# Moving adaLN's steps, the gate matmuls and the ScalarE and VectorE work of an RG-LRU behind other columns

## The chip, the cores and the metric

One Trainium2 chip, one core. The time is the device time of one execution in microseconds; lower is better. The whole network (two blocks, 256 positions) is one program, and all five engine programs run side by side, held together by semaphores alone.

## The reference

Two layers of a first block, then one layer of a second. What the change touches is the mixer of the first block's second layer (RG-LRU) and one matrix product of the second block that is computed far ahead, piece by piece (adaLN's `mod`):

```python
def rglru_mixer(h, w_in, conv_w, conv_b, w_a, b_a, w_x, b_x, lam, w_out):   # 10 blocks of 128 channels
    gate, xr = jnp.split(h @ w_in, 2, axis=-1)
    xr = causal_dwconv(xr, conv_w, conv_b)                # 4 taps
    r = sigmoid(blockwise(xr, w_a) + b_a)
    i = sigmoid(blockwise(xr, w_x) + b_x)
    log_a = -RG_C * r * softplus(-lam)
    a = exp(log_a)
    b = sqrt(-expm1(2.0 * log_a)) * (i * xr)
    hs = scan(a, b)                                       # h_t = a_t h_(t-1) + b_t
    return (gelu(gate) * hs) @ w_out
...
mod = c_act @ ada_w[l] + ada_b[l]                         # 1024 x 6144, of one row
```

## The kernel before

**Data.** Channels lie on the 128 partitions and the 256 positions along a row. Every weight matrix is read once from HBM in tiles of 128 x 1024 fp32 (512 KB): a "column" is 128 output channels by all 1024 inputs. A product in nearly full fp32 is made of three fast ones: each tile is split into a high part (`whi`, a ScalarE copy) and a low part (`wlo`, a VectorE subtraction), the input likewise (`hh`, `hl`), and TensorE adds hh·whi + hl·whi + hh·wlo, so a column is 24 matmuls of 128x128 by 128x256 into one PSUM bank. `project(w, [a, b])` makes two columns together: at each input tile k three matmuls of column a, then three of column b, so it needs both weights from its start.

**Order.** `weight_order` (line 113) lists all tiles as TensorE wants them, and SyncE starts their DMAs in that order into a ring of nine slots (`NR`); a DMA waits until TensorE is done with the tile nine places ahead. The high parts lie in seven buffers (`NS`). ScalarE and VectorE make the parts in the order of the list when their programs come to `feed(c)`: ScalarE up to place c+6 of the list, VectorE up to c+5 (`AHEAD` is 5, line 177; the loops stand at lines 1041 and 1565). What stands in an engine's program between two feeds runs before the later one. At the end of a residual both engines feed from the first weight of the next layer.

**adaLN.** Its matrix is 48 tiles in the same list, two for each of 24 steps. They aren't split: `mod_step` runs four narrow fp32 matmuls on each pair straight from the ring and adds into one PSUM bank that is held through a row of eight steps; at the eighth ScalarE copies the row to `mrow`. `mod_turn` is TensorE's four transposes of that copy into another bank, which VectorE adds to `mod`. The second row begins and ends in the RG-LRU: `ADA_RG` says behind which columns its eight steps come, and now the turn is asked for at each gate column and happens behind the first one after the eighth step.

**The RG-LRU.** Columns 10 to 19 of `rg_w_in` are the recurrent branch, 0 to 9 the gate. TensorE starts 10, 11, 12 on the unscaled input (`early`) while the norm's statistics are made. VectorE then makes the scaled input (`h_tiles`), lifts the three early columns and runs their taps (three each), and comes to the first `feed` of the layer only behind them. For each recurrent column m: ScalarE's `last_tap`, VectorE's `taps`; `ri(m)` is TensorE's two fp32 block matmuls and ScalarE's two sigmoids, and the table `RI` says behind which column it comes (places 0 to 9 are columns 10 to 19, places 10 to 19 the gates 0 to 9). GpSimd multiplies i by xr. ScalarE's `decays` are a tanh and two exps for each m, VectorE's `sizes` follow, ScalarE's `roots` (a square root for two m), VectorE's `scan`, ScalarE's `gelus` of the gate, VectorE's `times_gate`, ScalarE's `high_of_y`, VectorE's `low_of_y`. Each is put behind a gate column by a small table in the loops below, and the rest into the loop over the ten k of `rg_w_out`. That product runs k outermost over all eight outputs, so it takes all eight PSUM banks before its first matmul, the one of adaLN's row among them.

**Banks.** TensorE's `take` goes round the eight banks, leaves out the held one and waits until the last reader of the bank it comes to has given it back: for a recurrent column that is VectorE's last tap.

Sums go through a few helpers, so the profile has one line for each engine and operation: L470 TensorE, L1037 ScalarE, L1552 and L1558 VectorE, L1942 the scan, L573 the turn.

Of the kernel before, what the change touches and what calls it, by code (L numbers as in the profile page):

```python
# [79 lines left out]


ADA_IN = ((), (2, 5, 8, 11, 14, 17, 19, 21))
ADA_RG = ((5, 7, 9), (1, 3, 5, 7, 8))
YW = ((0, 2), (2, 2), (4, 2), (6, 4))


# [9 lines left out]

RI = ((), (), (), (), (), (), (0, 1), (2, 3), (4, 5), (6,), (7,), (8,), (9,)) + ((),) * 7

# [118 lines left out]
def build(nc, d, out):  # L221
    with ExitStack() as ctx:
# [241 lines left out]
        def tensor_program(e):  # L464
# [83 lines left out]
            def mod_step():  # L548
                n = ada["n"]
                ada["n"] += 1  # L550
                r, k = n // 8, n % 8
                if k == 0:
                    take(("ada", r))
                p = ps[where["ada", r]]
                for z in range(2):
                    c = number["ada_w", n, z]
                    landed[c % NR].wait_ge(e, c)
                    ada_dve.wait_ge(e, "sc32")
                    for y in range(2):
                        g = 2 * z + y  # L560
                        t = mm(p[32 * g:32 * g + 32, :], sc32[:, k, :], ring[c % NR][:, 4 * y:4 * y + 4, :], k == 0, k == 7)
                    t.then_inc(*through.up(c))
                if k == 7:
                    give(("ada", r), ada_act, r)
                    ada["late"] = r
# [118 lines left out]
            def conv_ffn(l):  # L684
                w = f"ffn_w_in{l}"
                n = 2 * l + 1
                early(n)
                for i, at in enumerate(EARLY[n]):
                    give(at, ff_dve, (l, "lift", i))
                project(w, [23, 2], n)  # L690
                give((w, 23), ff_dve, (l, "g", 1))
                give((w, 2), ff_dve, (l, "u", 2))
                for m in range(2, 22):
                    if m > 2:
                        project(w, [m], n)
                        give((w, m), ff_dve, (l, "u", m))
                    project(w, [m + 22], n)
                    give((w, m + 22), ff_dve, (l, "g", m))
                    if m in ADA_IN[l]:
                        mod_step()  # L700

                def also(m):
                    mod_turn()

                residual(2 * l + 2, f"ffn_w_out{l}", 22, pair(hidh[l], hidl[l]), lambda k: ff_dve.wait_ge(e, (l, "lo", k)), also)

            def rglru():
                def ri(m):
                    p, p2 = take(("r", m)), take(("i", m))
                    wab_in.wait_ge(e, "all")  # L710
                    rg_dve.wait_ge(e, ("x", m))
                    mm(p[:, 0:T], wab[:, m, :], xr[:, m, :]).then_inc(*rg_pe.up(("r", m)))
                    mm(p2[:, 0:T], wab[:, 10 + m, :], xr[:, m, :]).then_inc(*rg_pe.up(("i", m)))
                    give(("r", m), rg_act, ("r", m))
                    give(("i", m), rg_act, ("i", m))

                early(2)
                for m in range(3):
                    give(("rg_w_in", m + 10), rg_dve, ("lift", m))
                for m in range(3, 10):  # L720
                    if m == 3:
                        project("rg_w_in", [13, 14], 2)
                    elif m > 4:
                        project("rg_w_in", [m + 10], 2)
                    give(("rg_w_in", m + 10), rg_dve, ("x", m))
                    for i in RI[m]:
                        ri(i)
                    if m in ADA_RG[0]:
                        mod_step()
                for m in range(10):  # L730
                    project("rg_w_in", [m], 2)
                    give(("rg_w_in", m), rg_act, ("gate", m))
                    mod_turn()
                    if m in ADA_RG[1]:
                        mod_step()
                    for i in RI[m + 10]:
                        ri(i)
                outs = [take(("rg_w_out", m)) for m in range(8)]
                at = [(k, m) for k in range(8) for m in range(8)] + [(k, m) for m in range(8) for k in (8, 9)]
                for k, m in at:  # L740
                    c = number["rg_w_out", 0, k]
                    j = turn[c] % NS
                    low.wait_ge(e, c)
                    rg_dve.wait_ge(e, ("yl", k))
                    o, a, z = outs[m][:, 0:T], whi[j][:, m, :], wlo[c % NR][:, m, :]
                    mm(o, a, yh[:, k, :], k == 0, False)
                    mm(o, a, yl[:, k, :], False, False)
                    t = mm(o, z, yh[:, k, :], False, k == 9)
                    if k == 9:
                        t.then_inc(*rg_pe.up(("out", m)))  # L750
                        give(("rg_w_out", m), resid, (3, m))
                    elif m == 7:
                        t.then_inc(*through.up(c))
# [278 lines left out]
        def scalar_program(e):  # L1032
# [241 lines left out]
            def rglru():  # L1274
# [42 lines left out]
                def high_of_y(m):  # L1317
                    rg_dve.wait_ge(e, ("y", m))
                    act(yh[:, m, :], gate[:, m, :], ACT.Copy).then_inc(*rg_act.up(("yh", m)))
# [8 lines left out]
                for m in range(10):  # L1328
                    feed(tail("rg_w_in", m))
                    act(gate[:, m, :], out_of("rg_w_in", m), ACT.Copy).then_inc(*rg_act.up(("gate", m)))  # L1330
                    if m in ADA_RG[1]:
                        mod_step()
                    for i in RI[m + 10]:
                        ri(i)
                    decays({2: (0, 1, 2, 3), 3: (4, 5, 6), 4: (7, 8, 9)}.get(m, ()))
                    roots({5: (0, 2), 6: (4, 6), 7: (8,)}.get(m, ()))
                    gelus({7: (0, 1), 8: (2, 3, 4), 9: (5, 6, 7, 8, 9)}.get(m, ()))
                    if m > 7:
                        high_of_y(m - 8)
                for k in range(10):  # L1340
                    if k < 8:
                        high_of_y(k + 2)
                    if k == 9:
                        for m in range(8):
                            resid.wait_ge(e, (3, m))
                            gather(3, m)
                            high_of_h(3, m)
                    feed(number["rg_w_out", 0, k])
# [198 lines left out]
        def vector_program(e):  # L1547
# [322 lines left out]
            def conv_ffn(l):  # L1870
# [24 lines left out]
                for m in range(22):  # L1895
                    if m > 1:
                        feed(tail(w, m))
                    taps(zu_, "u", m, out_of(w, m) if m > 1 else zl[l][:, 2 * m, :], m)
                    if m:
                        feed(tail(w, m + 22))  # L1900
                    taps(zg_, "g", m + 22, out_of(w, m + 22) if m else zl[l][:, 1, :], m)
                    behind(m)
                    if m in ADA_IN[l]:
                        mod_step()
                behind(22)
                behind(23)

# [12 lines left out]
            def rglru():  # L1920
# [41 lines left out]
                        mod_step()  # L1962
                for m in range(10):
                    feed(tail("rg_w_in", m))
                    mod_turn()
                    if m in ADA_RG[1]:
                        mod_step()
                    sizes({2: (0, 1), 3: (2, 3, 4), 4: (5, 6, 7), 5: (8, 9)}.get(m, ()))
                    for i in {6: (0, 1), 7: (2,), 8: (3,), 9: (4,)}.get(m, ()):
                        scan(i)  # L1970
                    if m > 7:
                        times_gate(m - 8)
                    if m == 9:
                        low_of_y(0)
                for k in range(10):
                    if k < 5:
                        scan(k + 5)
                    if k < 8:
                        times_gate(k + 2)
                    if k < 9:  # L1980
                        low_of_y(k + 1)
                    if k == 9:
                        for m in range(8):
                            rg_pe.wait_ge(e, ("out", m))
                            add_to_x(3, m, ps[where["rg_w_out", m]][:, 0:T])
                            if m:
                                low_of_h(3, m - 1)
                        low_of_h(3, 7)
                    feed(number["rg_w_out", 0, k])
# [496 lines left out]
```

## Time and profile before

| | |
|---|---|
| median of 3 runs | 1162.47 us (1161.32 to 1162.50) |
| the profiled execution, its span | 1161.85 us, 1160.0 us |
| TensorE, VectorE, ScalarE busy | 94%, 72%, 55% of the span |
| mean granted TensorE clock | 0.976 of full |
| moved by DMA | 200.41 MB, 173 GB/s |

A busy TensorE is not TensorE at its peak: two matmuls overlap, so a record lasts about twice as long as the distance to the next. In a line of the timeline stand the start, the time from the first start to the last end of a run of like instructions, the engine, the operation, what is written and read, the count, and in brackets the idle time before it with what ended it.

### The profile page before, as it was taken

The page shows a single profiled execution, that of the slowest core. Times are in us where ns is not written, and L with a number is a line of the kernel's source. Part 1 is how long each engine was busy: PE and PEld are TensorE (multiplying, and loading weights), DVE is VectorE, ACT ScalarE, POOL GpSimd, SP SyncE. Part 2 cuts the span into 40 slices and gives each one's busy share as a digit, 9 for nine tenths or more (in the row PEclk, how much of TensorE's full clock was granted, in tenths as well). Part 3 has the DMA queues.
Part 4 walks back from the last instruction along what each step waited for, and adds up shares of the span by engine and source line. Part 5 has one row for each costly group of instructions (what it writes and reads, how often), then busy time and mean ns, then how long its engine had stood idle before and what let it go on. Part 6 is the DMA issues. An engine that isn't in the chain of part 4 may idle for free.

```text
span 1160.0 us, 21002 instructions
## 1 busy us (share of the span) xinstructions
PE 1091.7 (94%) x8588; PEld 1036.3 (89%) x8588; DVE 835.9 (72%) x1444; ACT 641.7 (55%) x1098; POOL 66.7 (6%) x79
## 2 busy tenths in 40 slices
PE   6996999999999979999999989899999979999996
PEld 6874999999987779999999978799989979999996
DVE  6465898887795397978787768998874587655442
ACT  6544576665564975756565675222333357875340
POOL 1130100000002001000000000000000011000010
PEclk9998999999999979999999989999999989999998
DMA  9366465556665844776776533222335255556551
GB/s 344 120 203 235 128 213 185 184 171 180 193 215 186 276 133 135 247 237 228 237 220 185 195 111 107 83 92 91 128 109 155 70 207 179 182 183 183 184 160 37
DMA packets 59857, 200.41 MB, mean 173 GB/s; under 512 B 6769, under 2 KB 11505, under 8 KB 59633
## 3 DMA queue, kind: packets, MB, share of 16 engines
q1 hardware_dynamic: 58032, 194.54, 51.7%
q10 hardware_dynamic: 1728, 4.53, 1.1%
q8 instruction: 68, 1.11, 0.4%
q14 instruction: 29, 0.23, 0.1%
HBM read 197.99 MB, written 1.05 MB: 172 GB/s over the span
## 4 chain that ended last, share of the span: by engine, by line
PE 81%; DVE 10%; ACT 6%; DMA 1%; issue 1%; ACTq 0%; SPq 0%; POOL 0%; DVEq 0%
PE ps L470 80%; DVE wlo L1552 2%; ACT whi L1037 1%; ACT L1037 1%; DVE xr L1558 1%; DMA ring<-pa_w_out 1%; DMA ring<-pa_w_in 1%; ACT xr L1037 1%; DVE cosT L1552 1%; ACT rr L1037 0%; DVE rst L1581 0%; DVE raw L1552 0%; DVE bks L1552 0%; DVE hl L1552 0%; ACT sc L1037 0%
## 5 line engine op out<-in xcount | busy, mean ns | idle before, releaser
L470 PE MATMUL ps<-hh,whi 128*128 128x256 f32 (+1 forms) x1656 | 481.1, 291 | 18.1 <-DVE wlo L1552 15.6
L470 PE MATMUL ps<-hh,wlo 128*128 128x256 f32 (+1 forms) x1656 | 471.3, 285 | 0.0
L470 PE MATMUL ps<-hl,whi 128*128 128x256 f32 (+1 forms) x1656 | 469.4, 283 | 0.0
L1552 DVE TENSOR_TENSOR wlo<-ring,whi 128x1024 fp32r<-128x1024 f32 (+1 forms) x313 | 376.1, 1216 | 73.8 <-ACT whi L1037 73.2
L1037 ACT ACTIVATE whi<-ring 128x1024 fp32r<-128x1024 f32 (+1 forms) x313 | 321.6, 1039 | 68.7 <-PE ps L470 52.6
L470 PEld LDWEIGHTS ps<-hh,whi 128*128 128x128 f32 x1656 | 316.6, 191 | 39.0 <-issue 31.2
L470 PEld LDWEIGHTS ps<-hl,whi 128*128 128x128 f32 x1656 | 317.1, 192 | 1.3 <-issue 1.0
L470 PEld LDWEIGHTS ps<-hh,wlo 128*128 128x128 f32 x1656 | 316.7, 191 | 0.0
L470 PE MATMUL ps<-hidh,whi 128*128 128x256 f32 x608 | 172.2, 283 | 0.0
L470 PE MATMUL ps<-hidh,wlo 128*128 128x256 f32 x608 | 172.1, 283 | 0.0
L470 PE MATMUL ps<-hidl,whi 128*128 128x256 f32 x608 | 172.1, 283 | 0.0
L470 PEld LDWEIGHTS ps<-hidh,whi 128*128 128x128 f32 x608 | 116.7, 192 | 0.8 <-issue 0.8
L470 PEld LDWEIGHTS ps<-hidl,whi 128*128 128x128 f32 x608 | 116.7, 192 | 0.0
L470 PEld LDWEIGHTS ps<-hidh,wlo 128*128 128x128 f32 x608 | 116.7, 192 | 0.0
L2329 POOL TENSOR_TENSOR sqa<-sqa,sqt 128x256 f32<-128x256 f32 x36 | 34.5, 960 | 950.3 <-ACT sqt L1037 950.3
L1037 ACT ACTIVATE sqt<-x 128x256 f32<-128x256 f32 x49 | 20.1, 414 | 74.0 <-DVE x L1552 36.3
L1558 DVE SCALAR_TENSOR_TENSOR zg<-ps,vec,zg 128x255 f32<-128x255 f32 x84 | 40.4, 481 | 23.7 <-ACT zg L1037 21.1
L1037 ACT ACTIVATE zg<-ps,vec 128x256 f32<-128x256 f32 x42 | 23.6, 562 | 44.7 <-PE ps L470 44.6
L1037 ACT ACT_TABLE_LOAD x35 | 44.9, 1283 | 6.1 <-issue 3.9
L1558 DVE SCALAR_TENSOR_TENSOR zu<-ps,vec,zu 128x255 f32<-128x255 f32 x80 | 38.5, 481 | 12.1 <-ACT zu L1037 9.5
L1037 ACT ACTIVATE zu<-ps,vec 128x256 f32<-128x256 f32 x40 | 22.5, 564 | 29.7 <-PE ps L470 21.0
L470 PE MATMUL ps<-yin,ring 128*128 128x256 f32 x160 | 38.6, 378 | 0.0
(360 smaller groups left out, 1354.3 us busy)
## 6 DMA issues: line engine op xcount, KB each, us to landing
ring<-ffn_w_in SPq DMA_DIRECT2D x88, 512.0 KB, 3.5
ring<-ffn_w SPq DMA_DIRECT2D x64, 512.0 KB, 4.4
ring<-w_in SPq DMA_DIRECT2D x51, 512.0 KB, 3.4
ring<-ada_w SPq DMA_DIRECT2D x48, 512.0 KB, 4.3
ring<-ffn_w_out SPq DMA_DIRECT2D x32, 448.0 KB, 3.3
ring<-rg_w_in SPq DMA_DIRECT2D x20, 512.0 KB, 4.4
ring<-pa_w_in SPq DMA_DIRECT2D x16, 512.0 KB, 7.5
ring<-ffn_w_out SPq DMA_DIRECT2D x16, 512.0 KB, 3.6
```

The source lines that it names most:

```text
L470: return e.matmul(o, l, r, start=start, stop=stop)
L1037: return e.activation(o, i, func, bias=bias, scale=scale, accum_out=acc)
L1552: return e.tensor_tensor(o, a, b, op)
L1558: return e.scalar_tensor_tensor(out=o, in0=a, scalar=s, in1=b, op0=op0, op1=op1)
L2329: e.tensor_tensor(sqa[:, :], sqa[:, :], sqt[:, m % 2, :], ADD).then_inc(*sum_g.up((n, m)))
```

## The change

The eight adaLN steps of the layer go behind columns 13, 14, 15, 16 and gates 6, 7, 8, 9; the turn goes out of the layer into `conv_ffn` (TensorE at m = 4, VectorE at m = 6). The block matmuls come in bunches of three, two, three, one and one. On ScalarE and VectorE decays, roots, gelus, sizes, scans and products come behind earlier gate columns, and more of them ahead of `rg_w_out`. Nothing is computed otherwise, and the instructions are the same in number.

```diff
-ADA_RG = ((5, 7, 9), (1, 3, 5, 7, 8))
+ADA_RG = ((3, 4, 5, 6), (6, 7, 8, 9))
...
-RI = ((), (), (), (), (), (), (0, 1), (2, 3), (4, 5), (6,), (7,), (8,), (9,)) + ((),) * 7
+RI = ((), (), (), (), (), (), (), (0, 1, 2), (3, 4), (5, 6, 7), (8,), (9,)) + ((),) * 8
...
@@ TensorE, conv_ffn
                     if m in ADA_IN[l]:
                         mod_step()
+                    if m == 4:
+                        mod_turn()
@@ TensorE, rglru
                     give(("rg_w_in", m), rg_act, ("gate", m))
-                    mod_turn()
                     if m in ADA_RG[1]:
@@ ScalarE, rglru
-                    decays({2: (0, 1, 2, 3), 3: (4, 5, 6), 4: (7, 8, 9)}.get(m, ()))
-                    roots({5: (0, 2), 6: (4, 6), 7: (8,)}.get(m, ()))
-                    gelus({7: (0, 1), 8: (2, 3, 4), 9: (5, 6, 7, 8, 9)}.get(m, ()))
-                    if m > 7:
-                        high_of_y(m - 8)
+                    decays({1: (0, 1, 2, 3), 2: (4, 5, 6), 3: (7, 8, 9)}.get(m, ()))
+                    roots({4: (0, 2), 5: (4, 6), 6: (8,)}.get(m, ()))
+                    gelus({6: (0, 1, 2), 7: (3, 4), 8: (5, 6, 7), 9: (8, 9)}.get(m, ()))
+                    for i in {7: (0,), 8: (1, 2), 9: (3, 4)}.get(m, ()):
+                        high_of_y(i)
                 for k in range(10):
-                    if k < 8:
-                        high_of_y(k + 2)
+                    if k < 5:
+                        high_of_y(k + 5)
@@ VectorE, conv_ffn
                     if m in ADA_IN[l]:
                         mod_step()
+                    if m == 6:
+                        mod_turn()
@@ VectorE, rglru
                     feed(tail("rg_w_in", m))
-                    mod_turn()
                     if m in ADA_RG[1]:
                         mod_step()
-                    sizes({2: (0, 1), 3: (2, 3, 4), 4: (5, 6, 7), 5: (8, 9)}.get(m, ()))
-                    for i in {6: (0, 1), 7: (2,), 8: (3,), 9: (4,)}.get(m, ()):
+                    sizes({2: (0, 1, 2), 3: (3, 4, 5), 4: (6, 7, 8, 9)}.get(m, ()))
+                    for i in {5: (0, 1), 6: (2, 3), 7: (4, 5), 8: (6, 7), 9: (8, 9)}.get(m, ()):
                         scan(i)
-                    if m > 7:
-                        times_gate(m - 8)
-                    if m == 9:
-                        low_of_y(0)
+                    for i in {7: (0, 1), 8: (2, 3), 9: (4, 5)}.get(m, ()):
+                        times_gate(i)
+                    for i in {8: (0,), 9: (1, 2)}.get(m, ()):
+                        low_of_y(i)
                 for k in range(10):
-                    if k < 5:
-                        scan(k + 5)
-                    if k < 8:
-                        times_gate(k + 2)
-                    if k < 9:
-                        low_of_y(k + 1)
+                    if k < 4:
+                        times_gate(k + 6)
+                    for i in {0: (3, 4), 1: (5,), 2: (6,), 3: (7,), 4: (8,), 5: (9,)}.get(k, ()):
+                        low_of_y(i)
```

## Rows read from the trace of the kernel before

**Rows 1.** The page: TensorE's busy time; the chain that ended last, by engine.
```profile
PE 1091.7 (94%) x8588; PEld 1036.3 (89%) x8588; DVE 835.9 (72%) x1444; ACT 641.7 (55%) x1098; POOL 66.7 (6%) x79
...
PE 81%; DVE 10%; ACT 6%; DMA 1%; issue 1%; ACTq 0%; SPq 0%; POOL 0%; DVEq 0%
```

**Rows 2.** Busy time by stretch: length, engines, then granted clock, DMA share, GB/s.
```profile
335.58:346.70 11.12, 9.84 (x81) 8.83 (x81) 10.79 (x26) 8.71 (x15) 0.00 (x0) 1.00 0.71 252
346.70:383.85 37.15, 34.80 (x237) 29.49 (x238) 20.99 (x30) 19.23 (x35) 8.55 (x9) 0.95 0.62 201
383.85:420.15 36.30, 26.95 (x201) 22.38 (x200) 21.04 (x34) 35.35 (x69) 0.73 (x1) 0.89 0.71 237
420.15:451.35 31.20, 31.20 (x240) 31.20 (x241) 26.01 (x46) 16.68 (x28) 2.51 (x4) 0.91 0.41 137
```

**Rows 3.** Timeline of VectorE, 323 to 347 us.
```profile
323.48 3.49 DVE L1552 TENSOR_TENSOR wlo<-ring,whi 128x1024 fp32r<-128x1024 f32 x3
...
329.89 1.22 DVE L1552 TENSOR_TENSOR wlo<-ring,whi 128x1024 fp32r<-128x1024 f32 x1
...
340.66 4.63 DVE L1558 SCALAR_TENSOR_TENSOR xr<-xl,vec,xr 128x255 f32<-128x255 f32 x9
345.33 1.22 DVE L1552 TENSOR_TENSOR wlo<-ring,whi 128x1024 fp32r<-128x1024 f32 x1
```

**Rows 4.** Timeline of TensorE, 335 to 347 us.
```profile
335.58 0.36 PE L470 MATMUL ps<-hh,whi 128*128 128x256 f32 x1 [0.62 <-DVE hl L1552]
...
344.36 1.06 PE L470 MATMUL ps<-ring,sc 128*32 128x512 f32 x8
346.70 0.36 PE L470 MATMUL ps<-hh,whi 128*128 128x256 f32 x1 [1.27 <-DVE wlo L1552]
```

**Rows 5.** TensorE behind its first wait of all, and at the turn and rg_w_out.
```profile
11.24 0.55 PE L470 MATMUL ps<-hh,whi 128*128 128x256 f32 x1 [11.24 <-DVE wlo L1552]
...
15.86 0.30 PE L470 MATMUL ps<-hh,whi 128*128 128x256 f32 x1
...
415.60 1.09 PE L573 MATMUL ps<-cst,mrow 128*128 128x128 f32 x4 [3.15 <-ACT mrow L1037]
420.15 0.55 PE L470 MATMUL ps<-yh,whi 128*128 128x256 f32 x1 [3.47 <-ACT gate L1037]
```

**Rows 6.** TensorE: block matmuls for two indices, at full and at half rate.
```profile
349.62 1.89 PE L470 MATMUL ps<-xr,wab 128*128 128x256 f32 x8
...
356.72 3.27 PE L470 MATMUL ps<-xr,wab 128*128 128x256 f32 x8 [2.35 <-DVE xr L1558]
```

**Rows 7.** The ring's DMAs, 345 to 400 us; TensorE, clock and DMA of one microsecond.
```profile
DMA to landing us min/median/max: 3.6/5.3/7.5
...
356.00:357.00 1.00, 0.28 (x1) 1.00 0.92 356
```

**Rows 8.** Timeline of ScalarE, 329 to 420 us.
```profile
329.47 1.28 ACT L1037 ACT_TABLE_LOAD   x1
331.48 0.42 ACT L1037 ACTIVATE rst<-rst 128x256 f32<-128x256 f32 x1 [0.72 <-DVE rst L1555]
...
383.85 0.50 ACT L1037 ACTIVATE xr<-rr,cf 128x256 f32<-128x256 f32 x1
...
390.90 2.00 ACT L1037 ACTIVATE whi<-ring 128x1024 fp32r<-128x1024 f32 x2
...
403.74 1.16 ACT L1037 ACTIVATE xr<-xr 128x512 f32<-128x512 f32 x2
...
414.87 0.58 ACT L1037 ACTIVATE mrow<-ps 128x512 f32<-128x512 f32 x1
...
418.44 1.63 ACT L1037 ACTIVATE gate<-gate 128x256 f32<-128x256 f32 x5
```

**Rows 9.** Timeline of VectorE: a scan, and the first low part of y.
```profile
404.87 0.69 DVE L1942 TENSOR_TENSOR_SCAN xr<-rr,ii 128x256 f32<-128x256 f32 x1
...
419.59 0.42 DVE L1552 TENSOR_TENSOR yl<-gate,yh 128x256 fp32r<-128x256 f32 x1
```

## The prediction

> **What bounds the kernel now.** I read the page first: TensorE is busy 94% of the span and makes 81% of the chain that ended last; VectorE has 10% of it, ScalarE 6% [rows 1]. So an edit that issues the same matmuls can only move TensorE's idle time and its clock. Next the busy time by stretch [rows 2], cut at four marks of the RG-LRU: first scaled matmul (335.58), column 16 (346.70), first decay on ScalarE (383.85), first matmul of rg_w_out (420.15) and its last (451.35). TensorE is short of full 1.3, 2.4 and 9.4 us in the first three, and not at all in the fourth. In the third ScalarE is busy 35.35 of 36.30 us: there it is the bound, and the granted clock is 0.89. Then engine by engine in order of time [rows 3 to 9]. The change aims at these stretches; the question is what is late in its place.
>
> I number the weights from column 10 of rg_w_in (index 0). `feed(c)` makes the high parts up to c+6 on ScalarE and the low parts up to c+5 on VectorE. AdaLN tiles count in this order but are not split.
>
> **Step 1, the look-ahead ends on an adaLN tile.** Now columns 10 to 15 are indices 0 to 5, and residual 2's last feeds make all their low parts. With ADA_RG[0] = (3, 4, 5, 6) the order is 10, 11, 12, 13, two tiles, 14 (index 6), two, 15 (9), two, 16 (12), two, 17 (15), 18, 19, gate 0. The last feed ends at index 5: the low part of 14 is not made. VectorE's next feed stands behind h_tiles, three lifts and nine taps: those run to 345.33, where the first low part starts [rows 3]. But project([13, 14]) takes both columns at each k, so its fourth matmul needs 14's low part. Two low parts fewer stand ahead of the statistics (3.49 for three, so 1.15 each), but VectorE then waits for ScalarE's root, and ScalarE has 14's high part (0.95) ahead of the table load: root at 329.47 - 1.15 + 0.95 + 1.30 = 330.6 for 331.48 [rows 3, 8]. So VectorE is 0.9 earlier: taps done at 344.4, low part of 14 at 345.6. TensorE, now at work from 335.58 after 0.62 idle [rows 4], would stand some 11 us. That is a new wait, the largest of the change.
>
> **Step 2, its clock.** The trace has this case: 11.24 us idle at the start, then the same 48 matmuls. They come 0.21 apart until 15.86 and 0.12 after it (22 and 26 of them, 4.6 + 3.1, and 0.3 for the last one's end [rows 5]): 8.0 us, the first part at half rate (1.2 of 2.4 GHz), where the three columns from 335.58 took 8.8, 2.9 each [rows 4]. Columns 13 and 14 end at 345.6 + 8.0 = 353.6.
>
> **Step 3, bare work to the last gate matmul.** Columns 15 to 19 and gates 0 and 1, 7 x 2.9 = 20.3; ten pairs of r and i, 0.77 each (1.89 for two indices, 0.35 of it under the next matmuls [rows 6]) = 7.7; adaLN steps for m = 3 to 6, 4 x 1.0 [rows 4] = 4.0. Sum 32.0, to 385.6. The pairs for 9 now lie behind gate 1, not gate 2; the number of adaLN steps ahead of them is the same (four).
>
> **Step 4, waits inside it.** (a) Column 15: VectorE waits for 13 (353.6), last_tap 0.5, three taps 1.5 (nine took 4.63 [rows 3]), low part 1.2: 356.8 against 355.6 on TensorE, 1.2. (b) Column 16 is index 12, in the ring slot of 13 (nine slots), so its DMA starts at 353.6. Landing took 3.6 at least, 5.3 in the median, in this stretch [rows 7]; I take 4.2, as the queue is empty. Then the high part 1.0, last_tap(4) behind it on ScalarE 0.5, taps 1.55, low part 1.2: 362.1 against 356.8 + 2.9 + 1.0 = 360.7, 1.4. (c) Column 17, three tiles later, at 1.5 us each (356 GB/s in a full microsecond [rows 7]: 0.524 MB / 356 = 1.47): landed 362.3, and through the same four steps 366.5 against 366.0 on TensorE, 0.5. (d) Bunches. Column 17 and the pairs 0, 1, 2 take 7 PSUM banks, adaLN's row holds the eighth, so column 18 takes 17's bank, which taps(7) frees. VectorE by then has in its queue, from 363.8: taps(5), low parts of 17, 18, 19, taps(6), low parts of gates 0, 1, 2, taps(7): 3 x 1.55 + 6 x 1.15 = 11.5, to 375.3; TensorE is there at 366.5 + 2.9 + 2.3 = 371.7: 3.6, and 1.6 for the half rate behind it (1.35 for the eight matmuls of row 356.72 against 349.62 alone [rows 6]). Sum 8.3. The bunch 5, 6, 7 waits for nothing: taps(9) is done when it ends. TensorE at 393.9, ScalarE's last sigmoid 0.8 later, 394.7, where the row of before has 383.85 [rows 8]. Bounds of this term: zero (all hidden), and 12, since now the stretch to 383.85 has 2.4 idle and 2.1 of half rate and each wait of mine could double.
>
> By the Trainium skill, page "DMA: Bandwidth & Descriptors", section "Bandwidth", SBUF's ports take at most 435 GB/s, an estimated 1.2 us a tile in place of my 1.5; (c) would go and the sum fall by 0.9. No full microsecond that I read in this stretch reaches it.
>
> **Step 5, ScalarE's chain from there.** By rows 8 (four decays, a load and a gate copy fill 383.85 to 390.90): ten decays at 1.34 with a load and what is between, 14.9; roots 1.3 + 5 x 0.52 = 3.9; gelus 0 to 7 1.3 + 8 x 0.3 = 3.7; gate copies 2 to 9, 2.2; high parts of gates 7, 8, 9 and of rg_w_out 0 to 5, 9 x 0.95 = 8.6; three high_of_y 1.2; the adaLN row's copy 0.5. Sum 35.0. This has to end before the first matmul of rg_w_out, since that takes all eight banks and the adaLN row's is the last: the copy now follows gate 9 and its feeds, while before it was at 414.87 and gate 9 came after [rows 8]. The turn (3.1 us of wait for that copy, 3.5 behind it [rows 5]) is gone, but the copy itself binds. Two waits come in: high_of_y(0) is at gate 7 and needs VectorE's scans 4 and 5 (1.1 each with their product [rows 9]), which stand behind gate 9's low part: ScalarE is there at 420.8, y(0) at 423.7, 2.9. At gate 8 high_of_y(2) needs scans 6 and 7 behind two low parts: 1.5. So 394.7 + 35.0 + 2.9 + 1.5 = 434.1. TensorE waits for gates 8 and 9 in this chain and then stands; yl(0), which released it before (419.59 + 0.42 [rows 9]), is long made. The start is 434.1 for 420.15: 13.95 later. Bounds of the two waits: 0 and 6.
>
> **Step 6, behind it.** rg_w_out takes 31.2 us with 5.3 of it at half rate [rows 2, 5]; TensorE comes from a stand again: no change. All scans but their products being done, VectorE has less to do there than now, hidden either way: 0. The turn's four transposes (1.09 at half rate now, no row at full; 0.55 by halving, between 0.2 and 1.1) go to ffn_w_in1's m = 4, where TensorE is full: +0.55. The bank given to VectorE at m = 6 is wanted seven takes on, at m = 8: 0. Nothing later gives time back: rows 1 say TensorE is the path.
>
> **Sum.** 13.95 + 0.55 = 14.5 on the profiled execution's 1161.85 (span 1160.0 and 1.85 around it), which is 0.6 under the median of 1162.47: 1176.35, given as 1176.5.
>
> **Rivals.** *A, the ladder closes up:* the 11 us stand is there, but step 4's waits lie beside each other and step 5's are not there. Then the last sigmoid is at 386.4, the start between 421.4 (chain 35.0) and 425.8 (39.4), so +1.8 to +6.2 with the turn: 1166. For it: VectorE is busy only 20.99 of 37.15 us in the second stretch [rows 2]. Against it: its work comes there in the order of its queue, not when it is wanted. *B, faster:* 14's low part is not what holds TensorE (it would have to be made ahead of the taps), so columns 13 and 14 run from 335 and only 15 waits, until 345.6. Then 345.6 + 30 of work + 0.8 + some 4.5 of waits and half rate as now = 380.9, the start between 415.9 and 420.3, and the turn's 7 us of standing before rg_w_out go. It wins if the last sigmoid falls before 384.6 with a chain of 35.0. Price -4 to +0.7, say 1160. Against it stands VectorE's program order. *C, worse:* the DMAs land at 5.3 and more and ScalarE's last_taps stand behind each high part, or a second clock drop comes at gates 8 and 9: +20 or more, 1183. *D:* nothing changes, because work only moves: needs 14.5 of hidden waits; I count it with A's lower edge.
>
> **Chances.** Forecast (1170 to 1181) 0.58, A 0.20, B 0.12, C 0.07, D 0.03. The likeliest's own range is 1170 to 1181. For 8 in 10 I leave out B, D and C's tail: 1164.5 to 1183. Within 0.2% (2.3 us, about what a measurement of this kernel tells from no change): D and edges of A and B, 0.06; faster 0.10; slower 0.84.
>
> **What would show it.** After: TensorE idle some 10 to 11 us behind the early columns, put down to VectorE's low part; half rate behind it; the first low part in the DVE rows right behind nine taps; a wait of 2 to 5 us ahead of column 18; the last sigmoid near 395; the adaLN row's copy right before the first rg_w_out matmul, near 434; stretch four again 31 us. If the first wait is under 3 us, step 1 is wrong and with it the sign; if it is there and the time is under 1168, steps 4 and 5 are.

## The result, and the profile after

The kernel after takes 1177.3 us (median of 4, 1175.3 to 1178.5), the kernel before 1162.1 in the same session (4 runs, 1161.3 to 1162.5): a ratio of 1.013, 95% interval 1.0112 to 1.0148. It is slower by 15. The profiled execution took 1175.3 (span 1173.5).

First the page, at the lines that answer to [rows 1]: busy time of TensorE, the chain, and the costliest matmul group (busy us, mean ns | idle before it, and how much of that VectorE's low parts ended).

```profile
PE 1092.5 (93%) x8588; PEld 1038.9 (89%) x8588; DVE 836.7 (71%) x1444; ACT 641.5 (55%) x1098; POOL 66.7 (6%) x79
...
PE 82%; DVE 9%; ACT 6%; DMA 2%; issue 1%; ACTq 0%; SPq 0%; POOL 0%; DVEq 0%
...
L470 PE MATMUL ps<-hh,whi 128*128 128x256 f32 (+1 forms) x1656 | 482.5, 291 | 34.9 <-DVE wlo L1553 29.3
```

TensorE's busy time grew by 0.8 us, the span by 13.5: it stands more. The third line says behind what: idle time ahead of this group is 34.9 us, 29.3 of it ended by a low part (before, 18.1 and 15.6).

Next the windows that answer to [rows 2], cut at the first scaled matmul, the end of columns 13 and 14, the first decay, the first matmul of rg_w_out and its last. (In [rows 2] the second mark lies one column later, at column 16, so the first two lines compare only together.)

```profile
333.96:352.86 18.90, 8.48 (x52) 8.14 (x56) 10.63 (x25) 4.93 (x10) 0.00 (x0) 0.64 0.21 78
352.86:393.21 40.35, 33.93 (x246) 29.00 (x246) 25.19 (x33) 24.48 (x42) 8.61 (x9) 1.00 0.60 210
393.21:433.18 39.97, 29.67 (x222) 25.46 (x220) 23.68 (x39) 34.76 (x69) 0.74 (x1) 0.86 0.67 222
433.18:464.40 31.22, 31.22 (x239) 31.22 (x240) 22.39 (x39) 16.20 (x28) 2.35 (x4) 0.91 0.42 136
```

Only the last is as it was (31.22 for 31.20). TensorE is short of full 10.4, 6.4 and 10.3 us in the other three, where it was 1.3, 2.4 and 9.4.

Which stretch of the program the time went to can be read without any choice of window from one pair of matmuls that stands once per sublayer: the sum of squares that opens each norm. It comes seven times; the third to the sixth are the four marks used here. TensorE's timeline after has them at

```profile
325.58 0.60 PE L470 MATMUL ps<-sqa,cst 128*128 128x256 f32 x2
...
468.25 0.67 PE L470 MATMUL ps<-sqa,cst 128*128 128x256 f32 x2 [1.36 <-POOL sqa L2329]
...
669.61 0.59 PE L470 MATMUL ps<-sqa,cst 128*128 128x256 f32 x2
...
979.66 0.59 PE L470 MATMUL ps<-sqa,cst 128*128 128x256 f32 x2
```

and before at 326.31, 455.05, 655.94 and 966.23. The distances, with those of every experiment (profiled executions, us; the medians are of several sessions, in which the kernel before had 1160.9 to 1162.1, so the ratios below are the ones to compare):

| kernel | to 1st mark | 1st to 2nd (RG-LRU) | 2nd to 3rd (conv_ffn) | 3rd to 4th | median us |
|---|---|---|---|---|---|
| before | 326.3 | 128.74 | 200.89 | 310.3 | 1162.1 |
| after | 325.6 | 142.67 | 201.36 | 310.1 | 1177.3 |
| b1 adaLN early only | 324.9 | 138.99 | 200.90 | 310.5 | 1171.8 |
| a1 after, one feed further | 327.3 | 130.32 | 201.34 | 308.8 | 1163.6 |
| b2 bunches only | 326.4 | 126.94 | 200.91 | 308.9 | 1157.5 |
| b3 turn only | 327.5 | 128.90 | 201.35 | 310.2 | 1162.8 |
| b4 bunches and tables | 326.8 | 130.09 | 200.92 | 312.5 | 1164.7 |
| b5 all but adaLN | 326.5 | 129.57 | 201.36 | 309.0 | 1161.9 |
| c1 after, y's waits gone | 325.0 | 142.98 | 201.33 | 310.2 | 1176.6 |
| d1 | 325.0 | 126.23 | 201.34 | 309.0 | 1160.0 |
| d2 | 324.8 | 126.28 | 201.35 | 309.0 | 1158.6 |
| e2 | 324.3 | 126.05 | 201.34 | 309.8 | 1158.7 |
| e1 | 325.2 | 121.51 | 201.37 | 313.1 | 1155.2 |
| f1 before with pairs | 327.3 | 123.54 | 200.91 | 309.0 | 1154.7 |

The RG-LRU is 13.93 us longer after, conv_ffn 0.47 (the turn), and the rest of the span scatters: its first part by 3 us and its third by 4, in kernels whose program is the same there, but for one feed in a1.

Inside the RG-LRU, TensorE's timeline (the rows that answer to [rows 4] and [rows 5]):

```profile
333.96 0.36 PE L470 MATMUL ps<-hh,whi 128*128 128x256 f32 x1 [0.86 <-DVE hl L1553]
...
344.97 0.58 PE L470 MATMUL ps<-hh,whi 128*128 128x256 f32 x1 [10.41 <-DVE wlo L1553]
...
352.79 1.92 PE L470 MATMUL ps<-ring,sc 128*32 128x512 f32 x16
356.49 0.36 PE L470 MATMUL ps<-hh,whi 128*128 128x256 f32 x1 [1.78 <-DVE wlo L1553]
...
361.01 0.36 PE L470 MATMUL ps<-hh,whi 128*128 128x256 f32 x1 [0.41 <-DVE wlo L1553]
...
366.50 0.36 PE L470 MATMUL ps<-hh,whi 128*128 128x256 f32 x1 [1.38 <-DVE wlo L1553]
...
375.07 0.38 PE L470 MATMUL ps<-hh,whi 128*128 128x256 f32 x1 [2.85 <-DVE xr L1559]
...
416.01 0.55 PE L470 MATMUL ps<-hh,whi 128*128 128x256 f32 x1 [3.83 <-DVE wlo L1553]
...
433.18 0.58 PE L470 MATMUL ps<-yh,whi 128*128 128x256 f32 x1 [6.47 <-ACT mrow L1038]
...
497.38 0.60 PE L573 MATMUL ps<-cst,mrow 128*128 128x128 f32 x4
```

In order: the first three matmuls of column 13, then a stand of 10.41 us in the middle of columns 13 and 14; columns 15, 16 and 17 each late by a low part; column 18 late by the taps that hold its bank; gate 8; rg_w_out behind the adaLN row's copy; and the turn's transposes, now at 497 at full rate.

VectorE's timeline there, for [rows 3]:

```profile
330.30 1.75 DVE L1582 RECIPROCAL rst<-rst 128x256 f32<-128x256 f32 x1 [1.86 <-ACT rst L1038]
...
339.03 4.63 DVE L1559 SCALAR_TENSOR_TENSOR xr<-xl,vec,xr 128x255 f32<-128x255 f32 x9
343.69 1.22 DVE L1553 TENSOR_TENSOR wlo<-ring,whi 128x1024 fp32r<-128x1024 f32 x1
353.57 1.52 DVE L1559 SCALAR_TENSOR_TENSOR xr<-ps,vec,xr 128x255 f32<-128x255 f32 x3 [8.65 <-ACT xr L1038]
```

The low part that TensorE waits for is the one right behind the nine taps. Then VectorE itself is idle for 8.65 us, waiting for column 13, which TensorE can't finish sooner. And ScalarE's timeline, for [rows 8]:

```profile
393.21 0.50 ACT L1038 ACTIVATE xr<-rr,cf 128x256 f32<-128x256 f32 x1
...
422.61 0.42 ACT L1038 ACTIVATE yh<-gate 128x256 fp32r<-128x256 f32 x1 [3.04 <-DVE gate L1553]
...
429.11 0.42 ACT L1038 ACTIVATE yh<-gate 128x256 fp32r<-128x256 f32 x1 [1.75 <-DVE gate L1553]
...
432.54 0.58 ACT L1038 ACTIVATE mrow<-ps 128x512 f32<-128x512 f32 x1
```

### The profile page after: what moved, and what is told of

Same layout as the page of the kernel before. It is cut to its first block, busy times and chain, and to the rows that moved or that the text cites. A ratio compares the mean times of both kernels' runs of the same rounds, so it can differ in the third digit from the quotient of the medians.

```text
span 1173.5 us, 21008 instructions
## 1 busy us (share of the span) xinstructions
PE 1092.5 (93%) x8588; PEld 1038.9 (89%) x8588; DVE 836.7 (71%) x1444; ACT 641.5 (55%) x1098; POOL 66.7 (6%) x79
## 4 chain that ended last, share of the span: by engine, by line
PE 82%; DVE 9%; ACT 6%; DMA 2%; issue 1%; ACTq 0%; SPq 0%; POOL 0%; DVEq 0%
PE ps L470 82%; DVE wlo L1553 2%; ACT whi L1038 1%; ACT L1038 1%; DMA ring<-pa_w_out 1%; DVE xr L1559 1%; DMA ring<-rg_w_in 1%; ACT xr L1038 1%; DMA ring<-pa_w_in 1%; DVE cosT L1553 1%; ACT rr L1038 0%; DVE rst L1582 0%; DVE raw L1553 0%; DVE bks L1553 0%; DVE hl L1553 0%
## 5 line engine op out<-in xcount | busy, mean ns | idle before, releaser
L470 PE MATMUL ps<-hh,whi 128*128 128x256 f32 (+1 forms) x1656 | 482.5, 291 | 34.9 <-DVE wlo L1553 29.3
L1038 ACT ACTIVATE sqt<-x 128x256 f32<-128x256 f32 x49 | 20.1, 414 | 75.1 <-DVE x L1553 37.4
L1559 DVE SCALAR_TENSOR_TENSOR zu<-ps,vec,zu 128x255 f32<-128x255 f32 x80 | 38.4, 481 | 14.4 <-ACT zu L1038 11.9
```

The source lines that it names most:

```text
L470: return e.matmul(o, l, r, start=start, stop=stop)
L1038: return e.activation(o, i, func, bias=bias, scale=scale, accum_out=acc)
L1559: return e.scalar_tensor_tensor(out=o, in0=a, scalar=s, in1=b, op0=op0, op1=op1)
```

## Experiments

**1. The look-ahead, cured and made alone.** a1 is the kernel after with one feed moved: VectorE makes 14's low part in residual 2.

```diff
-                    feed(first(n))
+                    feed(first(n) + (n == 2))
```

> The changed kernel with VectorE's last feed of residual 2 one place further, so that the low part of column 14's weight is made before the statistics and not behind the nine taps. Theory (the look-ahead wait costs what it looks like): TensorE's 10.4 us stand at 334.6 shrinks to the wait for column 15 (its low part stands behind taps(3), near 347.5), ScalarE's first decay moves from 393.2 to about 381, the start of rg_w_out from 433.2 to about 421; time 1163 to 1167. Rival (the ladder behind it and ScalarE's chain are the bound and the stand is hidden in them): the decays begin at 390 or later and the time stays above 1173.

Measured: 1163.6 (10 runs), ratio 1.0018 [1.0003, 1.0033]. The stand in columns 13 and 14 is gone; a shorter one is at column 15:

```profile
335.98 0.36 PE L470 MATMUL ps<-hh,whi 128*128 128x256 f32 x1 [1.19 <-DVE hl L1553]
348.65 0.55 PE L470 MATMUL ps<-hh,whi 128*128 128x256 f32 x1 [4.83 <-DVE wlo L1553]
```

The first decay is at 383.53 and rg_w_out starts at 423.51, each 2.5 later than expected. One low part, 1.2 us of VectorE, is worth 13 us of the 15 (1.0130 less 1.0018 of 1161).

b1 is the other way round: the kernel before with adaLN's steps early and nothing else.

```diff
-ADA_RG = ((5, 7, 9), (1, 3, 5, 7, 8))
+ADA_RG = ((3, 4, 5, 6), (3, 5, 7, 8))
```

> The kernel before with only the adaLN steps moved: ADA_RG = ((3, 4, 5, 6), (3, 5, 7, 8)); pairs, turn and the ScalarE and VectorE tables as they were. Theory: the look-ahead ends on an adaLN tile here too, TensorE stands 10 to 11 us ahead of the fourth matmul of columns 13 and 14 and runs at half rate behind it; waits for columns 15 and 16 as in the changed kernel, none of a bunch. First decay near 393 (383.85 before), 9 us later, time near 1171. Rival (the bunches and the tables cost the 13 us): within 3 us of before, 1159 to 1165.

Measured: 1171.8 (4 runs), ratio 1.0104 [1.0075, 1.0132]. The same stand, without the bunches, the new tables and the moved turn:

```profile
344.34 0.58 PE L470 MATMUL ps<-hh,whi 128*128 128x256 f32 x1 [10.44 <-DVE wlo L1552]
```

Steps 1 and 2 are shown from both sides.

**2. All but adaLN's place.** b5 is the kernel after with the old ADA_RG.

> The changed kernel with ADA_RG alone put back to ((5, 7, 9), (1, 3, 5, 7, 8)). Theory: adaLN's place is the whole loss. The first decay near 380, and ScalarE's copy of adaLN's row is out of the last place in its chain; rg_w_out starts between 413 and 419 for 420.15 before. Time 1156 to 1161, faster than before by 1 to 6 us. Rival (the waits of the chain weigh as much as the first stand): 1165 to 1170.

Measured: 1161.9 (10 runs), ratio 1.0007 [0.9996, 1.0018]: adaLN's place is the whole loss, but the gain that I expected besides (1156 to 1161) isn't there. The first decay is at 381.03, counted from the mark 3.0 earlier than before, and yet rg_w_out starts at 421.67, 1.3 later. The row's copy is done at 417.13 and doesn't hold it. The start waits 8.91 us. Two things are done just ahead of it: ScalarE's copy of gate 9 at 421.31, and a low part on VectorE at 421.65, to which the profile puts the wait down. Which of the two binds isn't shown.

**3. The bunches and the tables without the rest.** b4 takes RI and the tables of ScalarE and VectorE from after; adaLN and the turn are as before. b2 takes RI alone.

```diff
-RI = ((), (), (), (), (), (), (0, 1), (2, 3), (4, 5), (6,), (7,), (8,), (9,)) + ((),) * 7
+RI = ((), (), (), (), (), (), (), (0, 1, 2), (3, 4), (5, 6, 7), (8,), (9,)) + ((),) * 8
```

> The changed kernel with adaLN's steps and its turn back where they were: only the bunches of pairs and the ScalarE and VectorE tables are moved. Theory: the low parts of 13 to 15 are ready, no stand at 335; a PSUM bank wait in the first bunch (about 2 us for taps, then 1.5 ahead of column 18), but the last pair comes one gate earlier: first decay near 380, 3.6 us earlier; ScalarE's waits for y(0) and y(2), 4 to 5 us, take that back. Time 1159 to 1163. Rival (bunches and tables are themselves bad): 1168 or more.

> The kernel before with only the bunches, RI as in the changed kernel. Theory: the first decay follows gate 2's copy by the table of before, and TensorE reaches gate 2's end between 383 and 384 with or without the bunches (their bank waits, 1.8 and some 1 of half rate, take the place of 2.35 and of half rate at the same spot), so nothing moves by more than 1.5 us: 1160.5 to 1163. Rival (the bunches' bank waits are what made b4_bunches_tables 3 us slower than before): 1164 or more.

Measured: b4 1164.7 (6 runs), 1.0028 [1.0017, 1.004]; b2 1157.5 (7 runs), 0.9968 [0.9953, 0.9983]. Both outside what I expected, on opposite sides. The bunches are good and the tables bad. ScalarE's rows of b4 say how the tables cost:

```profile
413.88 0.42 ACT L1037 ACTIVATE yh<-gate 128x256 fp32r<-128x256 f32 x1 [2.46 <-DVE gate L1552]
417.31 0.58 ACT L1037 ACTIVATE mrow<-ps 128x512 f32<-128x512 f32 x1
```

and in b2 the copy comes at

```profile
414.24 0.58 ACT L1037 ACTIVATE mrow<-ps 128x512 f32<-128x512 f32 x1
```

The copy is 3.07 later in b4 (2.66 counted from the mark), although b4's first decay is 1.8 earlier: 2.46 is the wait for y(0), and three gelus and y(0)'s high part now stand ahead of the copy too. The RG-LRU is 3.15 longer (table above). The medians differ by 7, so some 3.6 more is in the third part of the span (312.5 for 308.9), where the two programs are the same. At least some of that is the execution's and not the kernel's: the profiled one is the slowest of b4's six, 1.3 over their median.

Why the bunches gain: before, the first pairs come behind column 16 and the second behind column 17. By the order in which `take` goes round the banks, index 2 then asks for the bank of column 16, which VectorE's taps of 16 give back: 2.35 of wait, then 1.38 of half rate over the pairs [rows 6]. In b2 that place reads

```profile
356.29 1.10 PE L470 MATMUL ps<-xr,wab 128*128 128x256 f32 x4 [1.78 <-DVE xr L1558]
357.32 1.79 PE L470 MATMUL ps<-ring,sc 128*32 128x512 f32 x8
```

The wait is 1.78, and half rate still follows it, over the adaLN step (1.79, where it takes 1.06 at full rate) and into the next column. So little is won there: counted from the mark the first decay is 0.74 earlier than before and the start of rg_w_out 0.71. The other 1.09 of the RG-LRU's 1.80 lie behind that start, at the granted clock. From the first matmul of rg_w_out to the next mark, before and then b2:

```profile
420.15:455.05 34.90, 33.51 (x259) 33.34 (x259) 28.30 (x51) 20.10 (x36) 4.43 (x6) 0.92 0.44 146
419.52:453.33 33.81, 32.43 (x258) 32.25 (x259) 28.19 (x51) 19.77 (x36) 4.42 (x6) 0.96 0.46 146
```

The turn's transposes stand behind a longer wait than before (3.95 for 3.15) and take 0.63 for 1.09. Why the clock was higher there isn't shown.

**4. The turn alone.** b3 is the kernel before with the turn in conv_ffn.

> The kernel before with only adaLN's turn moved into conv_ffn. Theory: the turn's waits (3.15 us for ScalarE's copy and, behind it, 3.47 for y) share one end, yl(0) at 420.0 and gate 9's copy, which the turn does not move; so rg_w_out starts at 420 all the same and the four transposes are paid in conv_ffn: no change to +1, 1161 to 1162.5. Rival (6.6 us of standing go with the turn): 1155 to 1158.

Measured: 1162.8 (11 runs), ratio 1.0008 [0.9998, 1.0017]. (The expectation ended at 1162.5.) The wait for the row's copy goes and all of it stands in the next one:

```profile
421.34 0.55 PE L470 MATMUL ps<-yh,whi 128*128 128x256 f32 x1 [7.61 <-ACT gate L1038]
```

The profile names ScalarE, but gate 9's copy is long done. What comes last is VectorE's yl(0), done at 421.20, 0.14 ahead of the start, as it was before (420.01 and 420.15 [rows 9]). The RG-LRU is 0.16 longer, conv_ffn 0.46. The turn costs its transposes and frees nothing, since yl(0) comes no sooner.

**5. ScalarE's waits for y.** c1 is the kernel after with high_of_y at gates 8 and 9 and the rest in rg_w_out's loop. On VectorE low_of_y(0) goes from behind gate 8's products to the head of gate 9, behind that gate's feed, and the other low parts of y into the loop.

```diff
-                    for i in {7: (0,), 8: (1, 2), 9: (3, 4)}.get(m, ()):
+                    for i in {8: (0,), 9: (1, 2)}.get(m, ()):
                         high_of_y(i)
...
+                    if m == 9:
+                        low_of_y(0)
```

> The changed kernel with high_of_y(0) behind gate 8, (1) and (2) behind gate 9 and the rest in the loop over k; VectorE's low_of_y(0) at the head of gate 9, so that ScalarE doesn't stand for y(0) and y(2) (3.04 and 1.75 us in the changed kernel) ahead of its copy of adaLN's row. Theory (ScalarE's chain binds and the waits lie in it): the first decay stays at 393, the copy and the start of rg_w_out come 4.5 to 5.5 us earlier, at 428; time 1171 to 1173.5. Rival (TensorE or VectorE has another bound there): the start moves by less than 2 us and the time stays above 1175.

Measured: 1176.6 (4 runs), ratio 1.0128 [1.0113, 1.0142]. The rival held. The copy is made at 429.88 for 432.54 (2.66 earlier; 2.04 counted from the mark, which c1 reaches 0.62 sooner), yet the start is at

```profile
432.86 0.55 PE L470 MATMUL ps<-yh,whi 128*128 128x256 f32 x1 [6.00 <-DVE yl L1553]
```

and VectorE's timeline says why:

```profile
428.02 0.95 DVE L1553 TENSOR_TENSOR gate<-gate,xr 128x256 f32<-128x256 f32 x2
428.89 3.49 DVE L1553 TENSOR_TENSOR wlo<-ring,whi 128x1024 fp32r<-128x1024 f32 x3
432.30 0.42 DVE L1553 TENSOR_TENSOR yl<-gate,yh 128x256 fp32r<-128x256 f32 x1
```

yl(0) stands behind scans, products and three low parts, and starts 0.56 before TensorE does. Counted from the mark, the start is 0.3 later than in after and the RG-LRU is 0.31 longer. Two things keep this from being a clean test. c1 itself put yl(0) behind the three low parts, where after has it ahead of them (made at 429.52). And its column 18 ran at half rate where after's didn't, so that its first decay is 1.04 later, counted from the mark (68.67 for 67.63). Counted from the first decay the start is 0.74 sooner (39.23 for 39.97): the wait changed its engine and gave that much. With yl(0) where after has it and ScalarE's waits gone the start could, by an estimate from these rows, be some 2 us sooner still (the copy is done at 430.46), which wasn't run.

**6. Towards a better kernel.** d1 is b5 with gelus spread over more gates and into rg_w_out's loop, high_of_y(0) at gate 8, and scans 7 to 9 in the loop. d2 also takes rg_w_out's banks one at a time.

```diff
-                outs = [take(("rg_w_out", m)) for m in range(8)]
+                outs = []
...
+                        if k == 0:
+                            outs.append(take(("rg_w_out", m)))
```

> The changed kernel with adaLN's steps back where they were (as b5_all_but_ada), and fewer things in ScalarE's chain ahead of rg_w_out: gelus 5 to 9 and high_of_y(1) on go into the loop over k, high_of_y(0) behind gate 8, scans 7 to 9 into the loop. Theory: in b5_all_but_ada the first decay is at 381.0 and rg_w_out starts at 421.7, 40.6 us later, of which 3.8 are waits for y and some 3 are gelus and high parts of y that nothing ahead of rg_w_out needs; without them the start is at 414 to 416: 1153.5 to 1157. Rival (what leaves the chain is paid again in the loop over k, where VectorE has 3.0 of work for TensorE's 2.9): 1159 to 1162.

> As d1_best, and TensorE takes the eight banks of rg_w_out one by one, each ahead of its first matmul, not all ahead of the first. Theory: the last banks to come back (gate 9's and adaLN's row's) are then wanted up to 2.5 us later; 0.5 to 2.5 us under d1_best, if it is a bank and not yl(0) or a low part that releases the first matmul there; if it is those, no change.

Measured: d1 1160.0, 0.9988 [0.9974, 1.0003]; d2 1158.6, 0.9983 [0.9969, 0.9997], 10 runs each. d1 missed its 1153.5 to 1157 and lies in the range of its rival, but not for the rival's reason: from the start to the next mark it takes 34.35 for 34.90 before, so nothing is paid again in the loop. The RG-LRU is 2.5 us shorter and no more: ScalarE's chain is short now, and rg_w_out waits for yl(0) at 416.83 and 416.70, so banks don't matter.

e2 is d2 with y(0)'s high and low parts made earlier; e1 is e2 with the pairs in five bunches of two.

```diff
+RI = ((), (), (), (), (), (), (), (0, 1), (2, 3), (4, 5), (6, 7), (8, 9)) + ((),) * 8
```

> As d2_best_lazy, with high_of_y(0) right behind gate 8's copy and low_of_y(0) behind gate 8's scan, where both stood behind three and four splits of weights. In d2_best_lazy rg_w_out started at 416.7, when yl(0) was made. Theory: the start moves to 413.5 to 414.5, where gate 9's copy is the last to come; 2 to 3 us under d2_best_lazy, runs near 1154 to 1156, median with the scatter of the clock 1155 to 1158. Rival (the low parts of rg_w_out's weights are late instead): no change.

> As e2_y0_early, with the block matmuls in pairs behind columns 17, 18, 19 and gates 0 and 1 in place of three, two, three, one, one. Theory: a pair and its column take 5 of the 7 free banks, so the bank waits in the first bunch (1.77 us, then half rate over column 18) go, and the first decay comes 1.5 to 3 us earlier: 1 to 3 us under e2_y0_early. Rival (four sigmoids at gate 1 stand ahead of the decays and take it back): no change.

Measured: e2 1158.7 (7 runs), 0.9973 [0.9962, 0.9983]; e1 1155.2 (5), 0.9945 [0.9932, 0.9959]. In e2 rg_w_out starts 4.8 us sooner than in d2, but yl(1) is made only 2.1 sooner:

```profile
411.89 0.35 PE L470 MATMUL ps<-yh,whi 128*128 128x256 f32 x1 [2.99 <-DVE yl L1556]
...
417.99 0.55 PE L470 MATMUL ps<-yh,whi 128*128 128x256 f32 x1 [3.00 <-DVE yl L1556]
```

What the start gave, the rest took: from it to the next mark e2 needs 38.41 for d2's 34.39, 3.00 of it the second wait and the rest the granted clock (0.91 for 0.94). Neither side of the expectation had this. e1's gain over e2 is the pairs': the first decay and the start come 2.2 and 2.1 sooner, counted from the mark, and the second wait is 1.50. So the last run put them into the kernel before, one tuple and nothing else:

> Before with one tuple changed: RI has pairs in five bunches of two behind tiles 7 to 11, where before has two, two, two and four single ones behind tiles 6 to 12; adaLN's steps, the turn and the tables of ScalarE and VectorE stay as before. Theory: of the best kernel so far (1155.2 for 1161.6) the pairs carry most. Then the first decay comes near 382 to 383 us, rg_w_out starts at 419 or before, no matmul of pairs waits over 1 us, TensorE's granted clock over the span is near 0.98, and the time is 1154.5 to 1157.5. Rival: the gain of the best kernel is that of the rewritten tables and of y(0)'s early start. Then rg_w_out starts at 420 again behind the same waits for the row's copy (3.95) and the last gate copy (3.93) that the three bunches alone had, and the time is 1157.5 to 1160, no less than with the bunches of three.

Measured: 1154.7 us (5 runs; before 1161.3, 9 runs), ratio 0.994 [0.9926, 0.9953]. The theory held, and the first decay came even sooner than expected, at 380.55: counted from the mark 4.28 earlier than before (53.26 for 57.54) and 3.54 earlier than in b2. Behind column 16's wait TensorE isn't idle once until then, and never at half rate, where before it lost 2.35 to the wait and ran at a granted clock of 0.95 [rows 2]:

```profile
347.70:380.55 32.85, 32.85 (x237) 28.61 (x238) 20.27 (x30) 18.94 (x35) 7.82 (x10) 1.00 0.71 229
```

```profile
380.55 0.50 ACT L1037 ACTIVATE xr<-rr,cf 128x256 f32<-128x256 f32 x1
```

That stretch took 37.15 before. All of it goes through ScalarE's chain to the start:

```profile
412.32 0.63 PE L573 MATMUL ps<-cst,mrow 128*128 128x128 f32 x4 [3.96 <-ACT mrow L1037]
416.88 0.55 PE L470 MATMUL ps<-yh,whi 128*128 128x256 f32 x1 [3.93 <-ACT gate L1037]
```

The start is 4.25 earlier than before, counted from the mark, and 0.95 more is won behind it, at a granted clock of 0.95 for 0.92. It is the same pair of waits as in b2, 2.64 earlier (3.5 counted from the mark), the second again ended by yl(0) (416.74); no pair waits for taps or banks. This is the best version found, level with e1 (the intervals overlap), and it needs none of the change's other edits.

## Why the prediction was right, step by step

The forecast was 1176.5 and the median is 1177.3; on the profiled execution 1176.35 against 1175.3. The profiled execution of after reaches the RG-LRU 0.73 us sooner than that of before (first mark, 325.58 for 326.31), which has nothing to do with the change; below it is added to after's times.

- **Step 1, right.** VectorE's low part behind nine taps starts at 343.69 + 0.73 = 344.4, as forecast; TensorE stood 10.41 (forecast some 11). The path to it is right too: ScalarE's root, 330.6 by forecast, starts at 329.86 + 0.73.
- **Step 2, right.** Columns 13 and 14 end 7.9 us after they resume (forecast 8.0), at 353.6 (forecast 353.6).
- **Step 3, 1.5 short.** From there to the last pair's end (392.80) is 39.94; less waits of 6.42 it is 33.5 for my 32.0. From start to next start the pairs take 8.4 instead of 7.7 (the bunch of three ahead of the wait 2.75, one index at the end 1.02, since nothing overlaps them there), the seven columns 21.1 instead of 20.3, the adaLN steps 4.0 as forecast.
- **Step 4, 1.9 too much.** Waits 1.78, 0.41, 1.38 and 2.85, where I had 1.2, 1.4, 0.5 and 3.6; the half rate of 1.6 behind the last didn't come. (a) to (d) are all there, at the engine I named; the sizes are off by up to 1 us each, and that they cancel (6.42 for 6.7) is luck. The DMAs show it: column 16's high part starts 3.6 us behind the end of columns 13 and 14, where I had 4.2, and column 17's 5.5 behind that, where three tiles at 1.5 gave 4.5. (The half rate of [rows 6] is 3.27 less 1.89, 1.38, not the 1.35 that I wrote.) The last sigmoid adds 0.4 and not 0.8. With step 3, which erred the other way: first decay 393.9 for 394.7.
- **Step 5, right in length.** From the first decay to the end of the row's copy is 39.9 us; less its waits for y, 3.04 and 1.75 (forecast 2.9 and 1.5), it is 35.1 for 35.0. The start is 433.9 for 434.1, so 13.8 later than before, for 13.95. The copy binds there and yl(0) was made before, as I wrote. What c1 adds is that the two waits for y aren't worth the 4.8 us that they last: taking them away as c1 does gave 0.7, because yl(0), put behind VectorE's last three low parts, then takes the place of the row's copy.
- **Step 6, right.** rg_w_out 31.22 for 31.20; the turn 0.60 in its rows, 0.46 in the distance of the marks, for 0.55.

The sum was 14.5; the marks give 13.93 + 0.47 = 14.4. That the two profiled executions differ by 13.45 (1175.3 less 1161.85) is the scatter of the other parts, 0.97 in after's favour, which the forecast could not know.

**The rivals.** A held that the waits close up; a1 shows that most of the stand does go through: undoing it shortens the RG-LRU by 12.35 (142.67 to 130.32), 11.35 of it ahead of rg_w_out. B rested on 14's low part not holding TensorE; a1 and b1 exclude it. What B had right is that the rest of the change could gain: with the stand cured, a1 is at +0.2%, and with adaLN's steps where they were, b5 is at no change. I had taken the bunches for a cost (step 4 d). Within after they cost their wait: b1, with the old pairs behind the same adaLN steps, waits 3.27 us from column 14 to its last pair, and after 6.42. But b1's decays stand one gate later, and the first comes at the same distance from the mark (67.5 and 67.6), so the bunches neither win nor lose up to there; nearly all of the 3.7 by which after's RG-LRU is longer than b1's arises behind it. No run takes the bunches alone out of after. In the program before, the bunches are worth 0.3%, as pairs 0.6%; for the pairs f1 shows why: the block matmuls no longer ask for a bank whose taps aren't done. I did not see that, since I priced each edit only on top of the early adaLN steps.

**What stays open.** Why the third part of the span takes 308.8 to 309.0 in some profiles, 309.8 to 310.5 in others and 312.5 or 313.1 in two, with the same instructions. It is the granted clock and no wait: TensorE's idle time there is 20.0 us in before, 20.1 in b2 and 20.1 in b4, at a clock of 0.97, 0.98 and 0.96. Why it is granted differently stays open. And how much of the tables' 7 us on b2 is more than the 3.15 shown.

## What to carry to other kernels

A look-ahead that counts tiles of two kinds is shortened by whichever kind needs no preparation: before moving such a tile ahead, list what the last feed in front of the next long stretch of the preparing engine still makes. Price every edit of a bundle alone against the old kernel too, since a good part can be buried under a bad one, as the bunches were. And when a wait is taken off one engine, read the queue of the next: here ScalarE's copy came 2 us sooner, and VectorE's yl(0), which the same edit had put behind three low parts, took its place.

## What the runs showed that I had not expected

The length of a wait does not fix the clock behind it. Column 18 ran at full rate behind 2.85 us idle in after (24 matmuls in 3.12 us), and in c1, with the same program up to there, at half rate for more than half of it behind 2.87 (4.41 us):

```profile
374.19:378.60 4.41, 4.41 (x25) 4.41 (x26) 1.55 (x1) 0.61 (x1) 0.47 (x1) 0.66 0.00 0
```

Gate 8 in after ran at half rate behind 3.83 (5.46 us at a granted clock of 0.50). In the kernel before, gate 8's column behind 2.73 idle was granted 0.64; in b2, behind 2.63, it was granted 1.00, and TensorE was about as busy in the 18 us ahead of each (15.27 and 15.37):

```profile
403.83:408.00 4.17, 4.17 (x24) 4.17 (x24) 3.47 (x7) 4.17 (x8) 0.00 (x0) 0.64 0.58 211
```

```profile
403.19:406.30 3.11, 3.11 (x28) 2.97 (x32) 2.65 (x6) 3.11 (x6) 0.00 (x0) 1.00 0.82 279
```

The first is TensorE's column in before, the second the same in b2. So a forecast should carry each half-rate term as a possible one, not a certain one. The ten runs of d1 also fall into two groups, five at 1156.7 to 1158.2 (mean clock 0.978 to 0.980) and five at 1161.8 to 1162.4 (0.973 to 0.975): one program, 5 us apart, so that a median of few runs can sit in either.
